# Weight ring slots placed at staggered byte offsets in a two-block transformer kernel on one core

## What is computed

```python
h = modulate(rms_norm(x, norm_mix_g[l]), sh_a, sc_a)     # 1024 features
... h @ ev_w_in / od_w_in ... @ w_out
x = x + g_f * swiglu(modulate(rms_norm(x, ...)), ffn_w_in[l], ffn_w_out[l])
...
z = rmsnorm(x, norm1_g[i]) @ w_in[i] + b_in[i]           # 12296 columns
x = x + jnp.square(jax.nn.relu(h2 @ w_ff1[i] + b_ff1[i])) @ w_ff2[i] + b_ff2[i]
x = x + jax.nn.sigmoid(h3 @ w_pe_gate[i]) * (p[i] @ w_pe[i])
```

## Time and profile before

| | |
|---|---|
| median of 3 runs | 2386.8 us (2385.46 to 2387.21) |
| profiled execution, first to last instruction | 2379.8 us |
| PE busy (matmul) | 2292.7 us, 96% |
| PE weight loads | 1954.9 us, 82% |
| DVE busy | 1496.3 us, 63% |
| ACT busy | 1028.4 us, 43% |
| DMA, read from HBM | 386.01 MB, 163 GB/s over the span |
| mean granted TensorE clock | 0.983 |

### The profile page before, as it was taken

One profiled execution on the slowest core, in us unless ns is written; L12 is line 12 of the kernel. 1 busy time (PEld: TensorE's weight loads), 2 busy tenths in 40 slices (PEclk: granted clock), 3 DMA queues, 4 the chain that ended last, 5 costly groups with the idle time before them and its releaser, 6 DMA issues.

```text
span 2379.8 us, 32080 instructions
## 1 busy us (share of the span) xinstructions
PE 2292.7 (96%) x13686; PEld 1954.9 (82%) x13686; DVE 1496.3 (63%) x1893; ACT 1028.4 (43%) x1256; POOL 0.2 (0%) x4
## 2 busy tenths in 40 slices
PE   6998989999998999999999999999999999999997
PEld 3775667777786878888998878999989987789997
DVE  4777543333346576765877767666678767767475
ACT  4255441121225265544663435444555534435343
POOL 0000000000000000000000000000000000000000
PEclk9999989999998999999999999999999999999999
DMA  8530034444422252555555544454555545345552
GB/s 329 206 148 1 36 126 193 159 195 159 159 106 107 88 125 89 195 188 205 215 185 178 184 171 160 178 191 178 179 188 196 187 176 198 141 178 183 177 183 101
DMA packets 61397, 389.12 MB, mean 164 GB/s; under 512 B 6600, under 2 KB 11080, under 8 KB 16072
## 3 DMA queue, kind: packets, MB, share of 16 engines
q1 hardware_dynamic: 61256, 387.08, 44.7%
HBM read 386.01 MB, written 1.05 MB: 163 GB/s over the span
## 4 chain that ended last, share of the span: by engine, by line
PE 86%; DVE 7%; ACT 4%; issue 2%; DMA 1%; SPq 0%; DVEq 0%; ACTq 0%
PE PS L509 23%; PE PS L511 23%; PE PS L510 23%; PE PS L615 5%; PE PS L613 3%; PE PS L864 1%; DMA raw<-chunks_in 1%; PE PS L1041 1%; DVE w_lo L1722 1%; ACT w_hi L1244 1%; ACT xn L1322 1%; PE PS L743 1%; PE PS L1023 1%; PE PS L703 1%; PE PS L768 1%
## 5 line engine op out<-in xcount | busy, mean ns | idle before, releaser
L1722 DVE TENSOR_TENSOR w_lo<-raw,w_hi 128x2048 fp32r<-128x2048 f32 x300 | 683.4, 2290 | 492.7 <-ACT w_hi L1244 491.6
L1244 ACT ACTIVATE w_hi<-raw 128x2048 fp32r<-128x2048 f32 x300 | 571.6, 1912 | 696.8 <-PE PS L511 323.8
L509 PE MATMUL PS<-x_hi_lo,w_hi 128*128 128x256 f32 (+1 forms) x1760 | 546.2, 310 | 9.7 <-DVE x_hi_lo L1787 5.2
L511 PE MATMUL PS<-x_hi_lo,w_lo 128*128 128x256 f32 (+1 forms) x1760 | 543.4, 309 | 0.0
L510 PE MATMUL PS<-x_hi_lo,w_hi 128*128 128x256 f32 (+1 forms) x1696 | 518.6, 306 | 0.0
L509 PEld LDWEIGHTS PS<-x_hi_lo,w_hi 128*128 128x128 f32 x1760 | 337.1, 192 | 36.3 <-issue 19.6
L511 PEld LDWEIGHTS PS<-x_hi_lo,w_lo 128*128 128x128 f32 x1760 | 337.0, 191 | 16.8
L510 PEld LDWEIGHTS PS<-x_hi_lo,w_hi 128*128 128x128 f32 x1696 | 325.1, 192 | 14.0
L509 PE MATMUL PS<-w_hi,x_hi_lo 128*128 128x512 f32 (+1 forms) x800 | 317.9, 397 | 15.6 <-DVE x_hi_lo L1787 10.8
L510 PE MATMUL PS<-w_lo,x_hi_lo 128*128 128x512 f32 (+1 forms) x800 | 313.5, 392 | 0.0
L511 PE MATMUL PS<-w_hi,x_hi_lo 128*128 128x512 f32 (+1 forms) x800 | 313.5, 392 | 0.0
(11 more groups left out here) (326 smaller groups left out, 2666.1 us busy)
## 6 DMA issues: line engine op xcount, KB each, us to landing
raw<-chunks_in SPq DMA_DIRECT2D x348, 1024.0 KB, 4.8
bias_ring<-brows_in SPq DMA_DIRECT2D x32, 256.0 KB, 5.0
G<-nrows_in SPq DMA_DIRECT2D x2, 1536.0 KB, 6.7
BIG<-rel_in SPq DMA_DIRECT2D x4, 512.0 KB, 7.7
free_b<-rel_in SPq DMA_DIRECT2D x4, 512.0 KB, 7.8
tabt<-tabs_in SPq DMA_DIRECT2D x1, 1536.0 KB, 11.7
X<-x_in SPq DMA_DIRECT2D x1, 1024.0 KB, 8.5
X<-ctx_in SPq DMA_DIRECT2D x1, 1024.0 KB, 10.5
```

Of the source, the lines that this page charges most:

```text
L509: pe.matmul(o, lhs[0], rhs[0], start=start, stop=False, **more)
L511: return pe.matmul(o, lhs[1], rhs[0], start=False, stop=stop, **more)
L1244: act.activation(w_hi[:, i % HI_RING, :], ring[:, n % RING, :], ACT.Copy).then_inc(*hi_ready.now(n))
L1722: dve.tensor_tensor(w_lo[:, c % RING, :], ring[:, c % RING, :], w_hi[:, i % HI_RING, :].bitcast(F32), ALU.subtract).then_inc(*lo_ready.now(c))
```

## The change

The slots get a pitch of 2056 floats instead of 2048, 32 bytes more, and the high ring begins 4 floats (16 bytes) into its tensor. In the built program `raw` still starts at byte 2176, so that raw and low slots start 0, 32, 64 and 96 bytes past a multiple of 128; `w_hi` starts at byte 35072 (274 times 128), and its slots start 16, 48 and 80 bytes past one. Each of the two tensors grows by 128 bytes, so everything placed behind them moves by 256 bytes and keeps its place against a multiple of 128 and of 256. The order of the instructions of every engine, their shapes and their waits stay as they were; only addresses differ.

```diff
+RING_STEP = CHUNK + 8
+HI_STEP = CHUNK + 8
+HI_LEAD = 4
...
-        raw_, raw_at = place("raw", RING * CHUNK)
-        wlo_, _ = place("w_lo", RING * CHUNK, F32R, raw_at)
-        whi_, _ = place("w_hi", HI_RING * CHUNK, F32R)
+        raw_, raw_at = place("raw", RING * RING_STEP)
+        wlo_, _ = place("w_lo", RING * RING_STEP, F32R, raw_at)
+        whi_, _ = place("w_hi", -(-(HI_LEAD + HI_RING * HI_STEP) // 32) * 32, F32R)
...
-        ring = raw_[:, :].rearrange("p (s n) -> p s n", s=RING)
-        w_hi = whi_[:, :].rearrange("p (s n) -> p s n", s=HI_RING)
-        w_lo = wlo_[:, :].rearrange("p (s n) -> p s n", s=RING)
+        ring = raw_[:, :].rearrange("p (s n) -> p s n", s=RING)[:, :, 0:CHUNK]
+        w_hi = whi_[:, HI_LEAD:HI_LEAD + HI_RING * HI_STEP].rearrange("p (s n) -> p s n", s=HI_RING)[:, :, 0:CHUNK]
+        w_lo = wlo_[:, :].rearrange("p (s n) -> p s n", s=RING)[:, :, 0:CHUNK]
```

## The result

The changed kernel takes **2395.6 us** (median of 4 runs, 2393.36 to 2396.12); the kernel before, measured along with it, 2386.13 us (median of 4, 2384.38 to 2387.21). The ratio is 1.0043, with a 95% interval of 1.0029 to 1.0058. The forecast was 2386.8 us, with a range up to 2392: the change costs 9.5 us, and the range did not hold it.

What follows compares the result with a forecast made beforehand. The prediction took PE, with 86% of the chain of waits, to bound the kernel. Matmuls, split and transfers summed to 0 + 0 + 0 on the 2379.8 us span, plus 7.0 us around it: 2386.8 us, range 2382 to 2392.

Steps and rivals of the forecast that it cites:

- What bounds the kernel: Chain of waits: PE has 86% of it, so only the pace of matmuls, or waits of PE, can show.
- Matmuls: Products that read a slot, 11472 counted: shifted starts taken to cost zero, bounds +45 and -68 us.
- The rival that has the streams colliding: TensorE's slot products: equal starts make accesses meet, the change ends it; in full 68 us faster, 2318.8 us; chance 0.07.
- The rival of a further fetch: Products of high slots: starts 16 past 32 bytes cost another fetch; in full 45 us, 2431.8 us; chance 0.06.
- 2 ns form: Further fetch at 2 ns for each of 5488 loads of high slots: 11 us, 2397.8 us.
- The split: ACT writes a high slot, DVE reads it beside the raw slot: taken as zero, at worst 0.2 us on the path.
- the transfers: DMA writes into raw slots, 29.4 us on the path: taken as zero, at most +5.5 us; chance of slower 0.03.
- 7.0 us lie around the span: The sum: 7.0 us added to the 2379.8 us span to reach the median of the runs, 2386.8 us.
- no effect: Whole kernel: no effect that can be seen, 2386.8 us with 4.8 us to either side; chance 0.84.
- What would show it: Signs in the profile: right at 120 and 227 ns steps, fetch at 121 ns or more, collision below 120 ns.

Runs made afterwards that it cites:

- m2: Small kernel without the model, TensorE alone: against m1, start varied by single floats, 4 to 128 stationary and 128 to 512 moving columns; 656.75 us in all.
- m1: Small kernel without the model, TensorE alone: 280 series of 24 matmuls with different starts of stationary and moving operand; 1197.31 us in all.
- e7: Kernel before, slots on 128 bytes, activations streamed by 1376 triples of 256-column products start 112 bytes past 128; 2362.94 against 2385.12 us, ratio 0.9907.
- m3: Small kernel without the model: slices walked in real product order, weights on 128 bytes, high and low activations each at eight starts; 1108.7 us in all.
- e3: The change with only raw and low slots shifted, high slots kept on 128 bytes; 2393.92 us against 2386.74 of the kernel before, ratio 1.0035.
- e2: The change with only high slots shifted, raw and low slots kept on 128 bytes; 2391.88 us against 2386.74 of the kernel before, ratio 1.0021.
- e1: Kernel before with only 256 bytes of padding put behind the high ring, slots unmoved; 2385.46 against 2386.74 us, ratio 0.9996.
- e5: Kernel before, slots unmoved, moving activations of all 256-column products shifted by 16 bytes; 2380.18 against 2384.86 us, ratio 0.9985.
- e8: As e7 with activations starting 16 bytes past 128 in place of 112; 2378.34 against 2385.12 us of the kernel before, ratio 0.9968.
- e9: Control, the layout of e7 with activations starting on 128 bytes; 2384.65 against 2385.12 us of the kernel before, ratio 1.0001.

## Why the prediction was wrong, step by step

**What bounds the kernel** was right: only the pace of matmuls could show, and it did.

**The step that failed is the term "Matmuls", taken as zero.** The prediction put it so: "I take zero", between +45 and -68 us. It measures -11.2 + 14.1 + 7.7 + 1.2 = +11.8 us, two effects of opposite sign that each lie far above what a measurement can tell. The zero rested on the gate products, which run at the same pace from both kinds of start. But they load four columns. m2 shows that four columns settle at 113.3 ns at all three starts tried beside 256 moving columns, where 128 columns range over 113 to 123 (m1). The one thing that could have shown the effect, a long load beside the stream, was missing from the row.

**The prediction had a view of it and argued it away.** The rival that has the streams colliding named the 6.5 ns that 128 stationary columns cost above four at 256 columns, and e7 won them: 120.0 to 113.3 ns. Against it the prediction said that the distance of load and stream "runs through all places during each load whatever their starts". m1 refutes what this was to show: with nothing else running, the starts alone move the step by up to 10 ns. The rival's own price, -68 us, had two faults. It gave the 6.5 ns to every shifted product, where an arbitrary shift wins 1.9 ns on average (m3) and only a chosen one all of it; and it gave them to the 512-column products too, for which both starts on 128 bytes are the best case already, with some 5 ns to lose. No row of before could show the second: every product that reads a slot with 512 columns had both operands there.

**The rival of a further fetch** (chance 0.06) has the total's sign and even, in its 2 ns form of 2397.8 us, nearly its size. Its mechanism is refuted: e3 has no slot at an odd multiple of 16 bytes and is 7.2 us slower, the loads did not lengthen but shortened by 4 ns, and the products that it was to slow by most, those with stationary high weights, became faster at 256 columns.

**The split and the transfers** were rightly taken as zero: 2292 and 1916 ns as before, 28.2 us of transfers where 29.4 were (the fourth piece, 7.1 us, came with no more idle time), and no visible price for starts at 32, 64 and 96 bytes.

**The sum and the range.** "7.0 us lie around the span" was read wrongly. In the runs of after the time is 1.8 us above the span (2395.42 to 2393.6); the rest was the spread between executions, which did no harm here. The range from 2382 to 2392 followed from 0.84 on "no effect". It was too much for a term whose bounds of +45 and -68 us came from no row with the shapes in question. That the miss is only 9.5 us is luck in part: the gain at 256 columns covers half of the loss at 512.

**What would show it.** The prediction asked for a pace below 120 ns as the sign of collisions and one above 121 as that of a fetch, in products of 256 columns only. For 512 columns it had only "start to start 227 ns" as the sign of being right, and that is where the loss was. Its sign that a collision would leave low products unchanged where their own slot did not move was wrong too: in e2 no low slot moved, and their steps changed (120.0 to 117.8 ns, 227.2 to 231.6).

## What to carry to other kernels

Where a run of matmuls sits at its pace, the places at which the stationary and the moving operand start are worth up to some 6% of a step at 256 columns and some 4% at 512, with no instruction changed. The best places differ by the number of moving columns, so shift the operand that only one kind of product reads, find the value with a small kernel that walks the slices as the real one does, and confirm it in the kernel itself. When a buffer grows, keep all that lies behind it in place to a multiple of 256 bytes (e1 lost nothing by that; by m1 a multiple of 512 changes no step at all), and when a term is bounded by a row, ask first whether the row has the shape in question on both operands.

## What the runs showed of the hardware

- **The load and the stream of TensorE are not independent in these products.** With TensorE alone at work and 128 stationary columns, 256 moving columns step at 113.3 to 123.3 ns and 512 at 226.7 to 237.5, by the starts alone; with 4 stationary columns 256 moving ones settle at 113.3. The stationary start alone is enough: with the moving operand at 0, moving it from 0 to 48 bytes turns 120.0 into 123.0 ns, and 226.7 into 233.3 at 512 columns. The Trainium skill, TensorE: Matmul & The Clock Gate, section Step-by-step: what each phase is for, says that loading the next weights doesn't take read bandwidth from the running matmul. For these float32r products that is not the whole story, by up to 10 ns a step. The Trainium skill, SBUF — State Buffer, section Specifications (TRN2), gives lines of 16 bytes; all slots in e2 and e3 start on such a line, and the step still moves.
- **The period is more than 128 bytes.** Shifting the moving operand by 128 bytes gives 118.4 and 232.4 ns, by 256 bytes 119.5 and 228.5, by 512 bytes nothing. In the model a shift by 256 bytes changed nothing that counts (e1), and one by 128 took 232.7 ns where 227 was (e5).
- **Moving both starts on by 32 bytes mostly changes nothing.** In m1's grid of pairs it leaves the step within 0.6 ns in 34 of 36 cases at 256 columns and 33 of 36 at 512; moving both by 16 bytes does so in 5 and 6 of 49.
- **A series falls into a rhythm.** After up to ten uneven steps it repeats a short pattern, and for some pairs there is more than one: 0/16 gave means of 113.3, 116.6 and 118.6 ns in m1 and m2. e8 and e9 show it in the model, 353.3 and 347.4 ns for the same starts of the wide form; what differs there is the products that ran before.
- **Still open:** the rule by which a pair of starts gets its rhythm, and why with 512 moving columns 4 stationary ones (231.7 ns) are slower than 128. That the reads of load and stream meet is the reading which fits m1 and the 256-column part of m2; it is not shown as the mechanism, and where in the chip they would meet, no run shows.
